# A mixture-of-experts layer: the last two experts' rows stay on chip, and TensorE adds them with one plane

## What is computed

```python
x = x + concat(ret, pool) @ w_out[l]
h2 = rms_norm(x, norm_ffn_w[l])
x = x + moe(h2, ...)          # top-4 of 32 clamped-SwiGLU experts, softmax gates
return rms_norm(x, norm_final_w)
...
def expert_block(args):       # for the tokens of one expert
    gu = xblk @ w_gu[e] + b_gu[e]
    x_glu = jnp.minimum(gu[:, :F], SWIGLU_LIMIT)
    x_lin = jnp.clip(gu[:, F:], -SWIGLU_LIMIT, SWIGLU_LIMIT)
    act = x_glu * jax.nn.sigmoid(SWIGLU_ALPHA * x_glu) * (x_lin + 1.0)
    return act @ w_down[e] + b_down[e]
```

## Time and profile before

| | |
|---|---|
| median of 3 executions | 1239.99 us (1237.2 to 1241.55) |
| profiled execution, its own time | 1238.21 us |
| span in the profile | 1236.4 us |
| granted TensorE clock, mean | 0.994 of full |
| TensorE busy with matmuls | 1139.9 us (92%) |
| VectorE busy | 1102.3 us (89%) |
| ScalarE busy | 922.3 us (75%) |
| GpSimd busy | 63.8 us (5%) |
| read from and written to HBM | 443.26 MB and 24.77 MB |

### The profile page before, as it was taken

The page is one execution under the profiler, slowest core; times in us unless marked ns, Lnnn a source line. Parts: engine busy times, 40 slices in busy tenths (PEclk is TensorE's granted clock), DMA queues, the critical chain, the costliest instruction groups (busy, mean ns, idle before and its releaser), DMA issues.

```text
span 1236.4 us, 40002 instructions
## 1 busy us (share of the span) xinstructions
PE 1139.9 (92%) x17556; PEld 884.0 (71%) x17557; DVE 1102.3 (89%) x806; ACT 922.3 (75%) x824; POOL 63.8 (5%) x70
## 2 busy tenths in 40 slices
PE   5999999999999999999999999999999999999982
PEld 3445556977788888778877777777777877888740
DVE  5855576999999999999999999999999999999948
ACT  4434445878888888888888888888888888888841
POOL 0110400000010000000000000000000000000000
PEclk9999999999999999999999999999999999999997
DMA  9605874999999999999999999999999999999964
GB/s 349 231 2 204 290 255 178 386 397 407 407 418 421 420 420 420 420 420 420 421 419 420 419 419 419 415 417 418 417 416 414 411 419 420 420 421 420 390 273 167
DMA packets 73255, 458.08 MB, mean 370 GB/s; under 512 B 10076, under 2 KB 10588, under 8 KB 23632
## 3 DMA queue, kind: packets, MB, share of 16 engines
q1 hardware_dynamic: 68480, 445.30, 88.3%
q0 software_dynamic: 3472, 8.21, 1.7%
q10 hardware_dynamic: 1152, 2.19, 0.5%
HBM read 443.26 MB, written 24.77 MB: 379 GB/s over the span
## 4 chain that ended last, share of the span: by engine, by line
PE 87%; issue 5%; DVE 5%; ACT 1%; DMA 1%; SPq 0%; DVEq 0%; ACTq 0%
PE ps L440 39%; PE ps L477 27%; PE ps L1146 8%; PE ps L433 7%; PE ps L1249 2%; PE ps L462 2%; DMA ring<-in_w_in_dram 1%; PE ps L1186 1%; DVE ring L419 1%; DMA arena<-in_norm_final_w_dram 1%; PE ps L1174 1%; DVE arena L1856 0%; DVE arena L1854 0%; DVE arena L1853 0%; PE ps L447 0%
## 5 line engine op out<-in xcount | busy, mean ns | idle before, releaser
L440 PE MATMUL ps<-arena,ring 128*128 128x88 f16 x12288 | 499.5, 205 | 38.1 <-issue 37.6
L440 PEld LDWEIGHTS ps<-arena,ring 128*128 128x128 f16 x12288 | 487.3, 100 | 43.8 <-issue 42.0
L419 DVE SCALAR_TENSOR_TENSOR ring<-ring 128x2048 f16<-128x2048 f32 x196 | 439.8, 2285 | 3.0 <-ACT ring L416 2.8
L419 DVE SCALAR_TENSOR_TENSOR ring<-arena,ring 128x2048 f16<-128x2048 f32 x156 | 354.2, 2287 | 34.1 <-ACT ring L416 34.0
L416 ACT ACTIVATE ring<-ring 128x2048 f16<-128x2048 f32 x196 | 364.4, 1907 | 9.3 <-DMA ring<-in_w_down_dram 4.5
L477 PE MATMUL ps<-ring,arena 128*88 128x512 f16 x1536 | 337.3, 379 | 3.9 <-issue 3.5
L416 ACT ACTIVATE ring<-arena 128x2048 f16<-128x2048 f32 x156 | 290.9, 1903 | 2.6 <-DMA arena<-in_w_down_dram 1.3
L477 PEld LDWEIGHTS ps<-ring,arena 128*88 128x88 f16 x1536 | 181.8, 120 | 145.7 <-issue 4.2
L524 ACT ACTIVATE arena<-ps,slot_gate 88x512 f32<-88x512 f32 x62 | 39.1, 680 | 102.6 <-PE ps L477 102.6
L433 PE MATMUL ps<-arena 128*128 128x88 f16 x2048 | 92.9, 205 | 10.7 <-issue 10.4
L433 PEld LDWEIGHTS ps<-arena 128*128 128x128 f16 x2048 | 84.6, 100 | 13.2 <-issue 13.0
(11 more groups left out here) (167 smaller groups left out, 590.6 us busy)
## 6 DMA issues: line engine op xcount, KB each, us to landing
ring<-in_w_gu_dram SPq DMA_DIRECT2D x130, 1024.0 KB, 19.5
arena<-in_w_gu_dram SPq DMA_DIRECT2D x125, 1024.0 KB, 18.0
ring<-in_w_down_dram SPq DMA_DIRECT2D x66, 1024.0 KB, 18.5
extra<-in_w_down_dram SPq DMA_DIRECT2D x31, 1024.0 KB, 19.3
arena<-in_w_down_dram SPq DMA_DIRECT2D x31, 1024.0 KB, 18.9
ring<-in_w_in_dram SPq DMA_DIRECT2D x4, 2048.0 KB, 12.5
arena<-planes SPq DMA_DIRECT2D x5, 1024.0 KB, 9.1
ring<-in_w_out_dram SPq DMA_DIRECT2D x2, 2048.0 KB, 8.5
```

Of the source, the lines that this page charges most:

```text
L419: return dve.scalar_tensor_tensor(split_of(slot)[:, 1, :], raw(r), SCALE_W, split_of(slot)[:, 0, :], ALU.mult, ALU.subtract)
L440: mm = pe.matmul(o, w[:, i, cols], src[:, j, k, :], start=start and n == 0, stop=stop and n == 2, skip_group_check=True)
```

## The change

- POOL scatters experts 0 to 29 only, and all that waited for 31 scatters waits for 30.
- Expert 30's rows are copied unscaled to `y_kept` in the slot `extra`; plane reads 6 and 7 go to slots 0 and 1 instead of `extra` and its neighbour, and wait for chunks 0 and 1 of the last down projection.
- `last_gates` makes a second matrix, `wg_kept`, for expert 30, and moves on VectorE from behind the routing to just ahead of the weights of expert 30. TensorE turns it as well, and ScalarE's copies of both turned matrices move ahead of its last two chunks.
- Expert 31's activations go to `actT_last` (the first buffer of `xT`) and its rows to banks 6 and 7 (`ROWS_LAST`); its down projection no longer waits for expert 30's rows.
- `fin_w` has a place of its own that is free after the second norm, and is loaded ahead of the loop, before `b_down`; VectorE waits for it at its first multiply.
- In `rest()` TensorE makes three adds per tile in a new order. VectorE adds both banks in one instruction, and takes planes of the next tiles between its other steps.

```diff
@@ sizes and places @@
+        wgT_kept = reg_p[:, 2816:2816 + S]
+        y_kept = extra[:, 0:1024]
+        wg_kept = reg_p[:, 4864:4864 + NT * CAP].rearrange("p (t c) -> p t c", t=NT)
+        actT_last = xT[:, 0]
-        fin_w = reg_h[:, 0:1024]
+        fin_w = reg_p[:, 0:1024]
...
-            return raw(raw_slot(E // 2, 0, DN_CH + i)).rearrange("p (k d) -> p k d", k=2)
+            return raw(raw_slot(E // 2, 0, DN_CH + i) if i < 6 else i - 6).rearrange("p (k d) -> p k d", k=2)
...
+        ROWS_LAST = ps[0:CAP, 6:8, :]
@@ SyncE and GpSimd @@
-                sp.wait_ge(scattered, 16 * (E - 1))
+                sp.wait_ge(scattered, 16 * (E - 2))
...
-                    sp.wait_ge(low_ready, nth(E, DN_CH + i) - SLOTS + 1)
+                    sp.wait_ge(low_ready, nth(E, DN_CH + i) - SLOTS + 1 if i < 6 else nth(E, i - 6) + 1)
...
-            for e in range(E - 1):
+            for e in range(E - 2):
                 add_rows(e)
@@ ScalarE @@
+            act.wait_ge(xn2_ready, NT)
+            act.dma_start(fin_w, norm_final_w.rearrange("(a d) -> a d", a=1).to_broadcast([P, D])).then_inc(fin_loaded, 16)
             act.dma_start(y_last[BD:P, :], b_down[0]).then_inc(tail_loaded, 16)
...
             high(E // 2, 0, 0)
-            finish_rows(E - 2, nth(E, 0))
-            act_high_part(E - 1)
+            act_high_part(E - 1, actT_last)
             high(E // 2, 0, 1)
+            act.wait_ge(wg_turned, 2)
+            act.activation(wgT, ps[:, 0, :], ACT.Copy).then_inc(wgT_ready, 1)
+            act.activation(wgT_kept, ps[:, 1, :], ACT.Copy).then_inc(wgT_ready, 1)
             high(E // 2, 0, 2)
             high(E // 2, 0, 3)
-            act.wait_ge(wg_turned, 1)
-            act.activation(wgT, ps[:, 0, :], ACT.Copy).then_inc(wgT_ready, 1)
+            act.wait_ge(chunk_used, nth(E, 0))
+            for half in range(2):
+                act_row(act, half, y_kept, 1.0 / (SCALE_A * SCALE_W)).then_inc(row_ready, 1)
...
             def rest():
                 norms[0] = 12
-                act.dma_start(fin_w, norm_final_w.rearrange("(a d) -> a d", a=1).to_broadcast([P, D])).then_inc(fin_loaded, 16)
                 for t in range(NT):
-                    act.wait_ge(acc_ready, 2 * t + 2)
+                    act.wait_ge(acc_ready, t + 1)
@@ TensorE @@
             mm.then_inc(wg_turned, 1)
+            for t in range(NT):
+                mm = pe.transpose(ps[0:CAP, 1, t * P:(t + 1) * P], wg_kept[:, t, :], ident)
+            mm.then_inc(wg_turned, 1)
             most = most_slots(pe)
-            pe.wait_ge(row_ready, 2 * E - 2)
             pe.wait_ge(act_ready, E)
...
             def rest():
...
+                def kept(t):
+                    add(t, wgT_kept[0:CAP, t * P:(t + 1) * P], y_kept[0:CAP], start=True)
+
+                def last(t):
+                    add(t, wgT[:, t * P:(t + 1) * P], y_last)
+
+                def plane(t):
                     pe.wait_ge(pair_loaded[2 * t + 1], 16)
+                    add(t, ident, pair(2 * t + 1)[:, 1, :], stop=True).then_inc(bias_done, 1)
+
+                pe.wait_ge(row_ready, 2 * E - 2)
+                kept(0)
+                kept(1)
+                pe.wait_ge(row_ready, 2 * E)
+                last(0)
+                plane(0)
+                last(1)
+                plane(1)
+                for t in (2, 3):
+                    kept(t)
+                    last(t)
+                    plane(t)
@@ VectorE @@
+                step(dve.tensor_tensor(wg_kept, ranks[:, 0:CAP].unsqueeze(1).to_broadcast([P, NT, CAP]),
+                                       rank1[:, E - 2, :].unsqueeze(2).to_broadcast([P, NT, CAP]), ALU.is_equal))
+                step(dve.tensor_tensor(wg_kept, wg_kept, gdense[:, :, E - 2].unsqueeze(2).to_broadcast([P, NT, CAP]), ALU.mult))
                 dve.sem_inc(routed, 1)
...
             next_onehot(1)
-            last_gates()
...
+            last_gates()
             stage(E // 2 - 1, 0)
             stage(E // 2 - 1, 1, last=True)
...
                 def add_last(t):
-                    for half in range(2):
-                        dve.wait_ge(bias_done, 2 * t + half + 1)
-                        xs = total[:, t, half * 512:(half + 1) * 512]
-                        dve.tensor_tensor(xs, ps[:, 2 * t + half, :], xs, ALU.add).then_inc(acc_ready, 1)
+                    dve.wait_ge(bias_done, t + 1)
+                    xs = total[:, t, :].rearrange("p (b c) -> p b c", b=2)
+                    dve.tensor_tensor(xs, ps[:, 2 * t:2 * t + 2, :], xs, ALU.add).then_inc(acc_ready, 1)
...
+                add_planes(0)
+                add_planes(1)
+                add_last(0)
+                add_planes(2)
+                finish(0)
+                add_last(1)
+                add_planes(3)
+                finish(1)
+                add_last(2)
+                finish(2)
+                add_last(3)
+                finish(3)
```

More of the change, by code:

```diff
@@ L470, in pe_gu, with pe_down @@
             return mm
-        def pe_down(pe, slot, f):
+        def pe_down(pe, slot, f, acts=actT, rows=ROWS):
             w = split_of(slot)
@@ L476, in pe_down @@
                 for n, (i, j) in enumerate(((0, 0), (0, 1), (1, 0))):
-                    mm = pe.matmul(ROWS[:, half, :], actT[:, j, f, :], w[:, i, col:col + 512], start=f == 0 and n == 0,
+                    mm = pe.matmul(rows[:, half, :], acts[:, j, f, :], w[:, i, col:col + 512], start=f == 0 and n == 0,
                                    stop=f == KD - 1 and n == 2, skip_group_check=True)
@@ L1061, in _ @@
             for half in range(2):
[L1062 removed]
+                act_row(act, half, y_last, 1.0 / (SCALE_A * SCALE_W), ROWS_LAST).then_inc(row_ready, 1)
             act.activation(std[:, 15, 0:1], eps_t[:, :], ACT.Sqrt).then_inc(root_table, 1)
@@ L1433, in rest, with add @@
             def rest():
-                pe.wait_ge(wgT_ready, 1)
-                for t in range(NT):
-                    pe.wait_ge(pair_loaded[2 * t + 1], 16)
-                    if t == 2:
-                        pe.wait_ge(row_ready, 2 * E)
-                    for half in range(2):
-                        pe.matmul(ps[:, 2 * t + half, :], ident, pair(2 * t + 1)[:, 1, half * 512:(half + 1) * 512],
-                                  start=True, stop=False)
-                    pe.wait_ge(tail_loaded, 16)
-                    pe.wait_ge(row_ready, 2 * E)
-                    for half in range(2):
-                        pe.matmul(ps[:, 2 * t + half, :], wgT[:, t * P:(t + 1) * P],
-                                  y_last[:, half * 512:(half + 1) * 512], start=False, stop=True).then_inc(bias_done, 1)
+                def add(t, w, rows, start=False, stop=False):
+                    for half in range(2):
+                        mm = pe.matmul(ps[:, 2 * t + half, :], w, rows[:, half * 512:(half + 1) * 512],
+                                       start=start, stop=stop)
+                    return mm
+                pe.wait_ge(wgT_ready, 2)
+                pe.wait_ge(tail_loaded, 16)
+                def kept(t):
[3 more added lines that the diff above has]
+                def plane(t):
+                    pe.wait_ge(pair_loaded[2 * t + 1], 16)
+                    add(t, ident, pair(2 * t + 1)[:, 1, :], stop=True).then_inc(bias_done, 1)
[11 more added lines that the diff above has]
+                    plane(t)
             ending(pe, most, rest, one, skip, last_added)
```

54 lines of the change are left out of this document (25 added, 29 removed).

## The result

The changed kernel takes **1230.21 us** (median of 7 runs, 1227.45 to 1233.71) against 1239.99 (7 runs, 1237.1 to 1243.2): ratio **0.9925**, 95% interval 0.9907 to 0.9942. The forecast was 1232.3 in a range of 1228.7 to 1237.6. The profiled execution has a span of 1228.4 us, 8.0 less than before.

A forecast was written before the change was run, and what follows sets the result against it. Bound by TensorE's matmuls up to 1182 us, then by the handover, the norm row's load and 28.6 us of VectorE work. Terms -8.0 and +0.3 gave -7.7 us, median 1232.3, range 1228.7 to 1237.6.

The forecast's parts named there:

- The sum: Whole kernel: -8.0 at the end plus +0.3 in the loop gives -7.7 us, as a median 1232.3 us.
- The handover: Around the last down projection: own buffer and banks for expert 31 let it end at 1193.8, 2.3 us earlier.
- TensorE's adds: After the last down projection: twelve adds, 22.2 us instead of 14.8; only the front exposed, tile 0's banks full at 1201.2.
- The reads: Plane reads near the end: held only by slots, queued behind `x_kept`; reads 1, 3, 5, 7 land by 1193.5, 1198.5, 1203.5, 1208.5.
- The pace of 358 GB/s: Rule against the plane reads' forecast pace of 424 GB/s: read 5 would land at 1206.1, the end moving 1.2 us.
- VectorE from 1201.2: VectorE's final work: planes 7.5, bank adds 4.8, finishes 4.4 and 7.0; 23.8 us in all, ending at 1225.0.
- the 7.16 and the 2.3: At the end: the norm row's 7.16 us load and the handover's 2.3 us, most of both claimed as kept gain.
- TensorE's four adds and two exposed roots: At the end, given back: four more TensorE adds, and finish(2) and finish(3) waiting 1.5 us each for ScalarE's square and root.
- The loop: Gate steps on VectorE grow from 1.65 to 2.8 us, norm row adds 1.24 to the queue; +0.3, bounds -1.65 to +4.0.
- The second rival: In the loop, gates 2.8 and norm row 1.24 arrive in full: 4.0 instead of 0.3, time 1236.0; chance 0.19.
- The clock rival: Clock falls to 1.2 GHz under TensorE's final adds, each 3.7 us instead of 1.85; time 1250; chance 0.03.

The follow-up runs named there:

- a_gates_early: Changed kernel with the five gate steps moved back behind the routing; stretch 42.53 us, median 1229.35 us, ratio 0.9928.
- a_row_late: Changed kernel with the norm row's load back in ScalarE's rest(), VectorE's wait still late; stretch 42.54 us, median 1232.54 us, ratio 0.9948.
- after_again: The changed kernel itself, run again beside other runs on one chip; stretch 42.54 us, median 1231.56 us, ratio 0.9933.
- a_roots_hidden: Changed kernel with VectorE's last adds of tiles 2 and 3 moved ahead of finish(1) and finish(2); stretch 39.51 us, median 1227.54 us, ratio 0.9901.
- b_row_early: Kernel before with the norm's row loaded ahead of the loop, VectorE's wait unmoved; stretch 43.26 us, median 1230.43 us, ratio 0.9941.
- a_reads_late: Changed kernel with plane reads held until VectorE made the last low half; stretch 46.43 us, median 1233.18 us, ratio 0.9955.
- b_wait_late2: Repeat, on another chip, of the kernel before with only the norm-row wait moved to VectorE's first multiply; stretch 46.84 us, median 1232.81 us, ratio 0.9947.
- b_wait_late: Kernel before with only VectorE's wait for the norm's row moved to its first multiply; stretch 44.17 us, median 1231.5 us, ratio 0.9941.
- a_best: Changed kernel with hidden roots, tile 0 served first by reads and TensorE, and early gate steps; stretch 37.91 us, median 1226.63 us, ratio 0.9893.
- after: The changed kernel in its first runs, against the kernel before; stretch 43.12 us, median 1230.21 us, ratio 0.9925.

## Why the prediction was right, and where it was not

- **The sum** (-7.7 us, median 1232.3): measured 1230.21, inside the range; the ratio's interval, on 1239.99, is 1228.5 to 1232.8. The span after, 1228.4, is the one forecast before the loop's 0.3.
- **The handover** (TensorE's last down projection ends at 1193.8): measured 1193.58; undone alone it is worth 2.0 to 2.6 us. Right, and as feared ScalarE's weight chunks 2 and 3 do wait for the turns: VectorE stood 1.37 us for the first of them at 1185.86, almost hidden from TensorE. One step was off without harm: "the high part (0.78) follows at once" (1178.1) had ScalarE wait 1.27 us for VectorE's product, until 1179.32. That product came at 1178.40, with the gate steps early (a_gates_early) at 1176.58; TensorE was busy with the loop until 1181.5 to 1181.9 in both.
- **TensorE's adds** (tile 0's banks full at 1201.2): 1200.46. Right; VectorE never waits for them on tiles 1 to 3.
- **The reads**: here a step failed. "The scatter of expert 29 is an expert's time older than that of 30, so nothing but slots holds the plane reads" is wrong. GpSimd's instruction for that scatter took 17.5 us instead of about 1, the scatter landed at 1180.58, and SyncE waited 12.7 us for it. That this cost nothing is luck, and the runs show why: reads issued before `x_kept` was complete landed behind it, however early they were issued. In a_gates_early, with a scatter of 0.91 us, they were issued from 1166.7 on, `x_kept` had landed at 1187.1 and the first read at 1189.6; its first add from a bank is at +18.69, as in a_row_late and after_again with scatters of 18.0 and 17.7. The landings themselves were forecast well: reads 1, 3, 5 and 7 at 1194.5, 1199.6, 1204.7 and 1209.7, each 1.0 to 1.2 us later than forecast, since `x_kept` was complete at 1189.4 and not at 1188.5. By the same delay VectorE left the planes of tiles 0 and 1 at 1200.96 and not 1199.8, and the forecast wait of 1.4 us for tile 0's bank is missing in this execution. There `x_kept` was complete 7.5 us behind the start of the turns of the gates; where it was 4.6 (a_roots_hidden) or 5.0 (after_again), the wait is there, 2.61 and 2.17 us, and the first add from a bank comes at +18.69. The first plane add started at 1192.04, as forecast. The pace of 358 GB/s stands in the Trainium skill (DMA: Bandwidth & Descriptors, Bandwidth) as what a core gets when both cores of a memory domain stream; the page says of its own higher figures that they hold for a single core. Here one core ran, and the reads went at 410 GB/s from 1195 to 1200, so the rule was no argument against the forecast.
- **VectorE from 1201.2** (23.8 us, end 1225.0): measured 24.01 from 1200.98. The joined add was put at 1.21 and took 1.22; the roots were put at 1.5 each and VectorE's idle time for them is 1.46 and 1.45.
- **What the 8 us are made of** is what the prediction had wrong, though its total was right. "Most of the 7.16 and the 2.3 is so kept; TensorE's four adds and two exposed roots are what is given back" names the parts but prices none of them against the old kernel. The runs do: the row off VectorE's path -7.9 (b_row_early), the handover -2.0 to -2.6, the earlier reads -3.3 to -3.9; given back, the roots +3.0 to +3.6 and the orders ahead of tile 0 +1.3 to +1.9. The parts were each undone alone and need not close: against the 42.54 of after_again they give -7.9 - 2.6 - 3.9 + 3.0 + 1.3 = -10.1 against a measured -8.6, and up to 0.8 of the gap is the longer hold in a_reads_late. The total came out because it was not built from the parts but forward from 1201.2, a point that TensorE sets. What this hid is that taking the row off VectorE's path gives nearly all: all else in the change nets 0.1 to 0.7 us in the stretch (against b_row_early), and 1.25 us in the times against the one moved line (b_wait_late2), where the intervals overlap.
- **The loop** (+0.3, bounds -1.65 to +4.0): the turns of the gates, right behind the loop's last matmul, start at 1181.87, before at 1181.84, and neither the gate steps nor the row's load put back changes the ratio by more than its interval. The second rival, at 4.0 us, gets no support; a term of 0.3 can't be tested against executions whose loops end 7 us apart.
- **The clock rival**: wrong for the changed kernel, and wrongly placed. "After waits of about 2 us at 1202 and 1208 it was still 1.00" took one execution for a rule; in b_wait_late2 a wait of 2.32 us went with a fall to 0.50, while one of 2.39 in b_wait_late did not. The wait of 2.56 us at the handover went with a fall in b_wait_late and b_wait_late2 and with none in the kernel before and b_row_early. What decides it is open. The price was put too high: an add at 0.50, the clock back only for its last part, took 2.95 us, not 3.7. The falls were seen in the old order alone, and the changed kernel has no such waits of TensorE.

## What to carry to other kernels

Before costing a change with several parts, cost its cheapest part alone: here a load that VectorE awaited long before its first use cost 7.9 us of stretch, of a whole change worth 8.0 to 8.6. Moving the wait alone gave 7.0 in one profiled execution and 4.3 in another, in which the clock fell twice; in the median times it gave 7.1 us on one chip and 7.8 of the change's 9.1 on another. When adds of several tiles go through two engines, let the first tile have everything first, and put another tile's add between a sum and the root that another engine takes of it; the two were worth 4.6 to 5.2 us in the stretch, 4.9 in the times with a_best (which also has the early gate steps). And before moving a read forward, ask what it lands behind: here reads issued 14 us earlier landed no earlier against `x_kept`.

## What the runs showed of the hardware

**A scatter that waits for a gap in VectorE.** GpSimd's row of expert 29's scatter in the changed kernel, and VectorE's rows beside it:

```profile
1156.59 17.48 POOL L504 DMA_INDIRECT planes<-arena,slot_row  x1 [28.00 <-ACT arena L529]
```

```profile
1159.19 4.49 DVE L423 SCALAR_TENSOR_TENSOR ring<-arena,ring 128x2048 f16<-128x2048 f32 x2
1163.59 0.88 DVE L526 SCALAR_TENSOR_TENSOR arena<-arena 128x704 f16<-128x704 f32 x1
1164.39 4.48 DVE L423 SCALAR_TENSOR_TENSOR ring<-arena,ring 128x2048 f16<-128x2048 f32 x2
1168.80 4.49 DVE L423 SCALAR_TENSOR_TENSOR ring<-ring 128x2048 f16<-128x2048 f32 x2
1173.20 0.88 DVE L516 TENSOR_SCALAR arena<-ps 128x704 f32<-128x704 f32 x1
1174.00 2.28 DVE L423 SCALAR_TENSOR_TENSOR ring<-extra,ring 128x2048 f16<-128x2048 f32 x1
```

VectorE has no gap from before the scatter's start on, and all its instructions have two inputs in SBUF until L516 at 1173.20, whose one input lies in PSUM; the scatter ends at 1174.07, with that instruction. In a_gates_early VectorE pauses for 0.90 us from 1155.83 to 1156.73, and the scatter takes 0.91 us from 1155.75:

```profile
1155.75 0.91 POOL L504 DMA_INDIRECT planes<-arena,slot_row  x1 [28.63 <-ACT arena L529]
```

```profile
1156.73 2.29 DVE L423 SCALAR_TENSOR_TENSOR ring<-arena,ring 128x2048 f16<-128x2048 f32 x1 [0.90 <-ACT ring L420]
```

a_best does the same (a gap of 0.91, a scatter of 0.91). Every profiled kernel with the gate steps late has a long one there, 17.3 to 18.1 us; none with them early has. But the gate steps are not needed for it. The changed kernel has a second one early in the loop:

```profile
331.44 18.72 POOL L504 DMA_INDIRECT planes<-arena,slot_row  x1 [27.97 <-ACT arena L529]
349.29 0.88 DVE L516 TENSOR_SCALAR arena<-ps 128x704 f32<-128x704 f32 x1
```

It too starts while VectorE goes without a gap and ends at 350.16, with VectorE's first instruction that reads PSUM (350.17). b_row_early, in the old order, has one of 18.73 us from 298.37, with the same end. The Trainium skill (SBUF — State Buffer, SBUF: two separate sides) says that a VectorE instruction with two SBUF inputs, and a GpSimd instruction that reads SBUF, lock one port pair against each other, each for its whole length; and, of VectorE's two-port modes, that GpSimd then can't write DMA descriptors. The rows fit this, and show more: a whole chain of back-to-back instructions of VectorE can hold a GpSimd DMA off for 17 to 18 us. It reads as if the lock were not passed on between two of them; the trace shows the waits and not the lock. Here the wait cost nothing, since the reads behind it queued behind `x_kept` anyway; where someone does wait for such a DMA, a pause of VectorE of 0.9 us may be worth having.

**The DMA engines at half.** At 1175 to 1185 us the share is 0.48 to 0.50 and 194 to 211 GB/s in the profiles before, of b_wait_late and of a_reads_late (from 1180), none of which issues a read of planes there. Yet SyncE's transfers are still under way. The trace's semaphore events show how: a transfer counts its semaphore up 16 times, and in this stretch the 16 come in two groups of eight. For the last row tile of `x_kept` in after, eight came at 1171.4 to 1172.1 and eight at 1185.0 to 1189.4, and the transfer is landed with the last. So one half of a transfer's shares runs some 13 to 17 us behind the other. Reads issued into this stretch use the free half: in a_best, which issues them from 1168.0, the share is 0.90 at 1175 to 1180, where it was 0.50. But they do not land sooner by it, for they land with the slower half: of after's read 0, eight came at 1185.0 to 1185.4 and the rest at 1187.5 to 1191.9, and the end of the reads is again at half share, 0.52 to 0.36 from 1203 to 1206. In the kernel before and a_reads_late, whose reads start on idle engines, the 16 of a read come within 1.3 us of each other. Why the two halves drift apart in the loop was not tried.
